# Two-layer model block on one Trainium2 core: weight splits given to GpSimd, convolution accumulated in PSUM

## The reference, cut to what matters

```python
def first_block(x, meta_tokens, ...):            # 512 tokens + 16 meta tokens, D = 1024
    n = _rms(h, norm_mix_w[l])
    z = n @ w_in[l]
    q, k, v, glu, g_att, g_conv = jnp.split(z, splits, axis=-1)
    o = _diff_attention(q, k, v, lam, cid)       # 8 heads, two softmaxes a head
    y_att = _rms(o, subln_w[l]) * (1.0 - lambda_init)
    u = glu[..., :CONV_CH] * jax.nn.sigmoid(glu[..., CONV_CH:])
    u = _causal_dwconv(u, conv_dw_w[l], conv_dw_b[l])       # 31 taps over positions, per channel
    u = jax.nn.silu(_layernorm(u, conv_ln_w[l], conv_ln_b[l]))
    y_conv = u @ w_conv_out[l]
    m = jax.nn.sigmoid(g_att) * y_att + jax.nn.sigmoid(g_conv) * y_conv
    h = h + m @ w_out[l]
    ...                                          # feed-forward part, then second_block
```

## Time and profile before

| what | value |
| --- | --- |
| median of 3 runs | 1806.2 us (1805.16 to 1809.17) |
| the profiled execution's own time | 1807.76 us |
| its span | 1806.0 us |
| PE busy | 1787.0 us (99%), 13222 matmuls |
| PE weight loads busy | 1687.2 us (93%) |
| DVE busy | 1403.3 us (78%) |
| ACT busy | 967.9 us (54%) |
| POOL busy | 164.6 us (9%) |
| granted PE clock over the span | 0.998 |

### The profile page before, as it was taken

The page is one execution under the profiler, slowest core; times in us unless marked ns, Lnnn a source line. Parts: engine busy times, 40 slices in busy tenths (PEclk is TensorE's granted clock), DMA queues, the critical chain, the costliest instruction groups (busy, mean ns, idle before and its releaser), DMA issues.

```text
span 1806.0 us, 31948 instructions
## 1 busy us (share of the span) xinstructions
PE 1787.0 (99%) x13222; PEld 1687.2 (93%) x13222; DVE 1403.3 (78%) x2464; ACT 967.9 (54%) x1894; POOL 164.6 (9%) x138
## 2 busy tenths in 40 slices
PE   9999999999999999999999999999999999999998
PEld 8999999978899989999889999999898999999987
DVE  5888898578756789969878996899357898689844
ACT  6223332568734446547556665667346566566632
POOL 0000000000000012011001211120000122122000
PEclk9999999999999999999999999999999999999999
DMA  5222222200132257566346876785332677577531
GB/s 193 96 75 93 94 86 80 94 24 25 64 107 73 80 136 165 133 160 144 108 117 146 173 159 139 157 170 127 117 94 71 127 167 161 139 156 168 124 117 70
DMA packets 247679, 213.42 MB, mean 118 GB/s; under 512 B 6646, under 2 KB 239919, under 8 KB 247534
## 3 DMA queue, kind: packets, MB, share of 16 engines
q1 hardware_dynamic: 180990, 178.34, 32.2%
q0 software_dynamic: 66528, 33.04, 14.9%
q10 hardware_dynamic: 16, 0.00, 0.0%
HBM read 209.26 MB, written 2.10 MB: 117 GB/s over the span
## 4 chain that ended last, share of the span: by engine, by line
PE 88%; DVE 6%; ACT 4%; DMA 1%; issue 1%; SPq 0%; DVEq 0%; ACTq 0%
PE ps L664 41%; PE ps L705 29%; PE ps L1313 6%; PE ps L1362 5%; DVE wlo L2350 2%; PE ps L893 1%; PE ps L1151 1%; PE ps L1126 1%; ACT p L1624 1%; ACT whi L1396 1%; DMA raw<-in_w_up_dram 1%; PE ps L1142 1%; PE ps L1154 1%; PE ps L918 1%; DVE y L2846 0%
## 5 line engine op out<-in xcount | busy, mean ns | idle before, releaser
L2350 DVE TENSOR_TENSOR wlo<-raw,whi 128x1024 fp32r<-128x1024 f32 (+1 forms) x363 | 438.7, 1214 | 203.9 <-ACT whi L1396 203.0
L1396 ACT ACTIVATE whi<-raw 128x1024 fp32r<-128x1024 f32 (+1 forms) x363 | 380.8, 1052 | 253.3 <-PE ps L664 107.1
L664 PE MATMUL ps<-nhi,whi 128*128 128x256 f32 (+3 forms) x1392 | 315.9, 290 | 1.5 <-DVE clo L2618 0.8
L664 PE MATMUL ps<-nhi,wlo 128*128 128x256 f32 (+3 forms) x1392 | 311.8, 288 | 0.0
L664 PE MATMUL ps<-nlo,whi 128*128 128x256 f32 (+2 forms) x1264 | 275.0, 287 | 0.0
L664 PEld LDWEIGHTS ps<-nhi,whi 128*128 128x128 f32 x1392 | 226.8, 189 | 5.2 <-DVE clo L2618 1.0
L664 PEld LDWEIGHTS ps<-nhi,wlo 128*128 128x128 f32 x1392 | 225.8, 189 | 2.1
L705 PE MATMUL ps<-thi,whi 128*128 128x256 f32 x784 | 225.2, 287 | 2.1 <-DVE wlo L2350 0.7
L705 PE MATMUL ps<-thi,wlo 128*128 128x256 f32 x784 | 221.6, 283 | 0.0
L705 PE MATMUL ps<-tlo,whi 128*128 128x256 f32 x784 | 221.4, 282 | 0.0
L705 PE MATMUL ps<-nhi,whi 128*128 128x256 f32 (+1 forms) x756 | 215.8, 285 | 0.0
(11 more groups left out here) (473 smaller groups left out, 3604.1 us busy)
## 6 DMA issues: line engine op xcount, KB each, us to landing
raw<-in_w_in_dram SPq DMA_DIRECT2D x90, 1024.0 KB, 5.9
raw<-in_w_up_dram SPq DMA_DIRECT2D x22, 1024.0 KB, 5.1
raw<-in_w_out_dram SPq DMA_DIRECT2D x20, 1024.0 KB, 5.1
s1t<-in_w_in_dram SPq DMA_DIRECT2D x49, 256.0 KB, 3.5
s1t<-in_w_in_dram POOLq DMA_DIRECT2D x49, 256.0 KB, 7.1
raw<-in_w_in_dram POOLq DMA_DIRECT2D x49, 256.0 KB, 4.7
raw<-in_w_down_dram SPq DMA_DIRECT2D x16, 512.0 KB, 3.4
raw<-in_w_conv_out_dram SPq DMA_DIRECT2D x4, 1024.0 KB, 5.2
```

The lines of the kernel that those rows point to most:

```text
L664: mm = eng.matmul(o, w, m[:, k, a:b], start=begins, stop=final and n == len(ks) - 1 and i == 2)
L1396: eng.activation(hi, raw, ACT.Copy).then_inc(*A.up("hi", s))
L2350: eng.tensor_tensor(lo, raw, hi.bitcast(F), ALU.subtract).then_inc(*V.up("lo", s))
```

## The change

Two things are done together, with what they need.

1. The subtraction `wlo = raw - whi` of slots 4 to 71 (`BY_GPSIMD`) is issued by POOL in place of DVE. PE and SP wait for POOL's signal there. POOL's three clearing instructions stand between these subtractions: `v` before that of slot 26, the two others before that of slot 58.
2. `conv_steps` keeps its running sum in PSUM banks 6 and 7 for 512 of the 514 positions; the last tap writes the result to `C` in SBUF. The first two positions are computed apart, for two channel blocks together, by two multiplies, one reduction and one addition. The transposed values move to the rotating pairs of banks, and `side.run(6)` becomes `side.run(7)` in the k, v and q tiles.

```diff
+        TAPS, EARLY_SUM = at("taps", [128, 2, 2, 31], F, o_ga + 8704), at("early_sum", [128, 2, 2], F, o_ga + 9728)
...
+        BY_GPSIMD = range(4, next(r for r, (u, _, _) in enumerate(slots) if u == first_ffn))
...
-        for kind in "kvq":
-            in_turn(3, *[(kind, h) for h in range(NH)])
-        turn_of[0] += 1
+        in_turn(3, *[("k", h) for h in range(NH)])
+        in_turn(3, ("v", 0), *[name for h in range(1, NH) for name in (("v", h), ("turn_v", h - 1))])
+        in_turn(3, ("q", 0), ("turn_v", 7), *[("q", h) for h in range(1, NH)])
+        turn_of[0] += 2
...
+        def low_in(s):
+            return G("lo", s) if s in BY_GPSIMD else V("lo", s)
...
                                 if n == c == i == j == 0:
-                                    on.wait_ge(V("lo", s))
+                                    on.wait_ge(low_in(s))
...
+            for n in range(2):
+                emptied([6 + n], V("tap", 6 + n, 30))
...
             def low(s):
+                if s in BY_GPSIMD:
+                    return
...
             def conv_steps(j):
+                fs, early = slice(2 * j, 2 * j + 2), [U[:, 2 * j:2 * j + 2, 14 + e:45 + e] for e in range(2)]
+                for e in range(2):
+                    on.wait_ge(V("u", 2 * j + 1), A("cv"), A("cf"), j and V("early", j - 1))
+                    eng.tensor_tensor(TAPS[:, :, e, :], early[e], cv[:, fs, 0:31], ALU.mult).then_inc(*V.up("early_taps", j, e))
+                yield
...
                 for tap in range(31):
                     for f in (2 * j, 2 * j + 1):
-                        src, c = U[:, f, 14 + tap:14 + tap + TQ], cv[:, f, tap:tap + 1]
+                        src, c = U[:, f, 16 + tap:16 + tap + T2], cv[:, f, tap:tap + 1]
+                        z = bank_dst(6 + f % 2)[0]
...
-                            eng.scalar_tensor_tensor(C[:, f, :], src, c, C[:, f, :], ALU.mult, ALU.add).then_inc(*V.up("tap", f, tap))
+                            eng.scalar_tensor_tensor(z if tap < 30 else C[:, f, 2:TQ], src, c, z, ALU.mult, ALU.add) \
+                                .then_inc(*V.up("tap", f, tap))
...
-                side.run(6)
+                side.run(7)
...
+            for s in BY_GPSIMD:
+                u = slots[s][0]
+                if s == slots.index((12, BY_COL[0], False)) + 2:
+                    on.wait_ge(T("keys"), A("square_x", 0))
+                    eng.memset(V_[:, 0, :], 0.0).then_inc(*G.up("meta"))
...
+                hi, lo, raw = split_views(s)
+                on.wait_ge(A("hi", s))
+                eng.tensor_tensor(lo, raw, hi.bitcast(F), ALU.subtract).then_inc(*G.up("lo", s))
```

More of the change, by code:

```diff
@@ L828, in turn_values @@
             def turn_values(h):
-                src = VT[h % 2]
-                on.wait_ge(A("vt", h), *free(6, 7))
+                src, b = VT[h % 2], 2 * PAIR["turn_v", h]
+                on.wait_ge(A("vt", h), *free(b, b + 1))
                 for t in range(4):
-                    turned = eng.transpose(P[:, 3072 + 128 * t:3200 + 128 * t], src[:, NM + 128 * t:NM + 128 * t + 128], ident)
+                    turned = eng.transpose(P[:, 512 * b + 128 * t:512 * b + 128 * t + 128], src[:, NM + 128 * t:NM + 128 * t + 128], ident)
                 turned.then_inc(*T.up("turn_v", h))
-                eng.transpose(P[0:NM, 3584:3712], src[:, 0:NM], ident).then_inc(*T.up("turn_vm", h))
-                emptied([6], A("v", h))
-                emptied([7], A("vm", h))
+                eng.transpose(P[0:NM, 512 * b + 512:512 * b + 640], src[:, 0:NM], ident).then_inc(*T.up("turn_vm", h))
+                emptied([b], A("v", h))
+                emptied([b + 1], A("vm", h))
             for h in range(NH):
@@ L1552, in turn_values @@
             def turn_values(h):
+                b = 1024 * PAIR["turn_v", h]
                 on.wait_ge(T("turn_v", h))
-                eng.activation(V_[:, 1:5, 128 * h:128 * h + 128], P[:, 3072:3584].rearrange("p (t c) -> p t c", t=4), ACT.Copy) \
+                eng.activation(V_[:, 1:5, 128 * h:128 * h + 128], P[:, b:b + 512].rearrange("p (t c) -> p t c", t=4), ACT.Copy) \
                     .then_inc(*A.up("v", h))
                 on.wait_ge(T("turn_vm", h), G("meta"))
-                eng.activation(V_[0:NM, 0, 128 * h:128 * h + 128], P[0:NM, 3584:3712], ACT.Copy).then_inc(*A.up("vm", h))
+                eng.activation(V_[0:NM, 0, 128 * h:128 * h + 128], P[0:NM, b + 512:b + 640], ACT.Copy).then_inc(*A.up("vm", h))
             for h in range(NH):
@@ L2511, in conv_steps @@
             def conv_steps(j):
+                fs, early = slice(2 * j, 2 * j + 2), [U[:, 2 * j:2 * j + 2, 14 + e:45 + e] for e in range(2)]
[3 more added lines that the diff above has]
+                yield
+                on.wait_ge(V("early_taps", j, 0), V("early_taps", j, 1))
+                eng.tensor_reduce(EARLY_SUM, TAPS, AX.X, ALU.add).then_inc(*V.up("early_sum", j))
+                yield
+                on.wait_ge(V("early_sum", j))
+                eng.tensor_tensor(C[:, fs, 0:2], EARLY_SUM, cv[:, fs, CB:CB + 1].to_broadcast([128, 2, 2]), ALU.add) \
+                    .then_inc(*V.up("early", j))
+                yield
                 for tap in range(31):
                     for f in (2 * j, 2 * j + 1):
-                        src, c = U[:, f, 14 + tap:14 + tap + TQ], cv[:, f, tap:tap + 1]
+                        src, c = U[:, f, 16 + tap:16 + tap + T2], cv[:, f, tap:tap + 1]
+                        z = bank_dst(6 + f % 2)[0]
                         if tap == 0:
-                            on.wait_ge(V("u", f), A("cv"), A("cf"))
-                            eng.tensor_scalar(C[:, f, :], src, c, cv[:, f, CB:CB + 1], ALU.mult, ALU.add).then_inc(*V.up("tap", f, 0))
+                            on.wait_ge(V("u", f), A("cv"), A("cf"), V("tap", f - 2, 30) if j else V("u", 1))
+                            eng.tensor_scalar(z, src, c, cv[:, f, CB:CB + 1], ALU.mult, ALU.add).then_inc(*V.up("tap", f, 0))
                         else:
                             on.wait_ge(V("tap", f, tap - 1))
-                            eng.scalar_tensor_tensor(C[:, f, :], src, c, C[:, f, :], ALU.mult, ALU.add).then_inc(*V.up("tap", f, tap))
+                            eng.scalar_tensor_tensor(z if tap < 30 else C[:, f, 2:TQ], src, c, z, ALU.mult, ALU.add) \
+                                .then_inc(*V.up("tap", f, tap))
                         yield
@@ L2523, in conv_steps @@
                     if f == 1:
-                        on.wait_ge(V("tap", 0, 30), V("tap", 1, 30))
+                        on.wait_ge(V("tap", 0, 30), V("tap", 1, 30), V("early", 0))
                         eng.tensor_tensor(LNS, C[:, 0, :], C[:, 1, :], ALU.add).then_inc(*V.up("sum", 1))
                     elif f > 1:
-                        on.wait_ge(V("sum", f - 1), V("tap", f, 30))
+                        on.wait_ge(V("sum", f - 1), V("tap", f, 30), V("early", f // 2))
                         eng.tensor_tensor(LNS, LNS, C[:, f, :], ALU.add).then_inc(*V.up("sum", f))
@@ L3498, in gpsimd_program @@
             eng.memset(U[:, :, 0:30], 0.0).then_inc(*G.up("pad"))
[L3499 to L3503, removed]
+            for s in BY_GPSIMD:
[3 more added lines that the diff above has]
+                    eng.memset(V_[:, 0, :], 0.0).then_inc(*G.up("meta"))
+                elif s == slots.index((28, BY_COL[0], False)) + 2:
+                    for i in range(2):
+                        on.wait_ge(T("gate", 15))
+                        eng.memset(AT[i][:, 4, :], 0.0).then_inc(*G.up("at_rows", i))
+                hi, lo, raw = split_views(s)
+                on.wait_ge(A("hi", s))
+                eng.tensor_tensor(lo, raw, hi.bitcast(F), ALU.subtract).then_inc(*G.up("lo", s))
             def first_sum(n):
@@ L3556, in first_sum @@
                         on.wait_ge(V("second_sum", sevens[n - 2]), V("lo", slot_of[sevens[n - 2], 1]))
-                    on.wait_ge(V("lo", raw2_read))
+                    on.wait_ge(low_in(raw2_read))
                     eng.dma_start(S1T[n % 2], plan[u][0][:, 0:4, 128:256]).then_inc(*QUARTER_IN[n % 2].up("unit", u))
```

## The result

| | before | after |
| --- | --- | --- |
| median of 4 runs each | 1807.41 us | 1819.25 us |
| lowest to highest | 1805.16 to 1809.17 us | 1816.71 to 1822.72 us |
| profiled execution, its span | 1807.76, 1806.0 us | 1816.71, 1814.9 us |

The ratio is 1.0067, 95% interval 1.0046 to 1.0089: slower by about 12 us, between 8 and 16 by the interval. The forecast was 1818.6 us, 12.4 above the 1806.2 of that time.

The account below looks back on a forecast made before the run. PE alone was taken to set the pace up to about 345 us, then PE, DVE and ACT closely geared in attention. Holds of 9.6 + 1.0 + 1.8 = 12.4 us on 1806.2 gave 1818.6 us, range 1804.0 to 1823.5.

Parts of the forecast that it names:

- The first 345 us, 0: Before attention PE is never idle, so freeing DVE of 54 subtractions and moving the convolution to PSUM gains 0.
- POOL's subtraction, 2.25 us: Duration of one low-part subtraction on POOL, estimated at 2.25 us, between 1.6 and 2.7.
- The disputed term: In attention, POOL's SBUF reads hold DVE's two-input instruction for d = 2.1 us; less 0.5, 1.6 a head, 9.6 for six.
- the room of 0.5: In each attention head, 0.5 us before DVE's reciprocal, won back from the hold because DVE's low part is gone.
- First head 1.0, end 1.8: Hold costs 1.0 us in attention's first head and 0.9 for each of two subtractions at attention's end.
- the sum of 12.4: Total predicted loss in us from holds in attention: 9.6 + 1.0 + 1.8.
- The gain of 0.2 us a head: In attention, DVE without its low part lets PE start 0.2 us sooner a head, 1.2 us for six.
- Taps in PSUM, 0 to 0.1 us: In the convolution, writing the sum to PSUM adds 0 to 0.1 us a tap; effect on the kernel's time 0.
- The moved transposes, 0: Transposed values in rotating bank pairs cost 0: pairs are claimed again two tiles later, copies take under 1 us.
- no hindrance: Rival for attention: POOL and DVE read side by side or lose little; 1805.0 us, the same; chance 0.33.
- POOL as the bound: Rival: POOL's subtraction outlasts a 5.9 us tile, PE waits at 51 slots; at 6.5 us, +31, 1837 us; chance 0.02.
- taps over 1 us: Rival: PSUM taps over 1 us each end after the gates begin their layer norm, so PE waits; chance 0.02.

Follow-up runs that it names:

- the first two experiments: Changed kernel with POOL subtracting only up to slot 57: 1806.97 us, ratio 1.0000; changed kernel with every subtraction on DVE, convolution in PSUM: 1806.27 us, ratio 1.0001.

## Why the prediction was right

- **The first 345 us, 0**: right for the 54 subtractions and for the convolution, and shown by the first two experiments apart. The last tap is 22 us earlier and nobody waited for it.
- **POOL's subtraction, 2.25 us** (between 1.6 and 2.7): 2.40 beside taps, 2.36 in attention. That I came so near is in part luck: I had added a price for each read, and the multiply with one read takes 2.8 us, longer than the subtraction with two, so the instruction's time is not made up in that way. The estimate from the Trainium skill's figure (GPSIMD Engine Reference, section 3.1; 2.2 us for this size) was about as near as mine.
- **The disputed term, d = 2.1 less 0.5 = 1.6 us a head**: right as a mechanism, and 1.5 in size. `ast` is held by 2.03 us; the room of 0.5 shows as the difference between 2.03 a head with DVE's own subtraction kept and 1.5 without it. Of my place for it only this differed: one row takes the whole hold, and the rows behind it run as before.
- **First head 1.0, end 1.8**: 1.5 and 1.3, and that they make up the sum is luck. The 1.5 of the first head are PE's clock, which I had not foreseen; the hold there adds nothing that the trace shows. It can: with taps in SBUF the first head's chain goes through an `ast` of 1.68 us. At the end I charged two subtractions with 0.9 each. One holds `rcol` by 2.17 us (2.33 against 0.16), the other `mlo` by 0.85; the room there was not as I had placed it. So the sum of 12.4 compares with 10.5 us of POOL's.
- **The gain of 0.2 us a head** from a DVE without the low part: measured by itself, 14.65 to 14.46.
- **Taps in PSUM, 0 to 0.1 us**: 0. **The moved transposes, 0**: 0.9 us, once. PE waits 0.67 us for ACT's copy of the last query tile at about 257 us, because the next tile now takes the same pair of banks; the wait is in every kernel with the moved transposes and absent where the transposes stay in banks 6 and 7. It is too small to show in the medians.
- **The rivals**: no hindrance fell by the row of 2.25 us; POOL as the bound by PE's 304.3 busy us of 305; taps over 1 us by the row of 748 ns.

What the prediction lacked was the alternative that a scheduler would look for: in the same head there is a stretch behind the maximum in which DVE reads PSUM or is idle, and the same subtraction costs nothing there. In short: the mechanism of the main term and its size a head (1.6 forecast, 1.5 measured) were right, and the rest of the agreement, 12.4 against 12.05, is two terms that I had left out (0.9 and 1.5 us) and an execution that began 0.85 us earlier.

## What to carry to other kernels

Work taken off an engine under a PE that never idles is worth nothing, however much of it there is: 54 of 68 subtractions moved here without a trace in the time, though they held DVE there too. When elementwise work with SBUF inputs goes to GpSimd, list what VectorE does in the 2.4 us behind its release: a one-column instruction with both inputs in SBUF was held for 2.03 us here, nearly all of the 2.36, so let the GpSimd instruction wait for a point at which VectorE reads PSUM or is idle, or cut it into pieces, which left 0.6 of the 1.5 us a head here. Look for an instruction whose row is ten times its usual length and ends with one of another engine; the median of its group hides it if only some are held. Compare the granted clock stage by stage too, before a difference is charged to the change.

## What the runs showed of the hardware that I had not expected

- POOL's one-input multiply on 128x1024 took 2.8 us, longer than the two-input subtraction (2.37), but held DVE for 0.72 us only.
- An integer `TENSOR_SCALAR` of 128x4, SBUF to SBUF, took 2.24 us beside POOL's subtraction, where it takes 0.17.
- The hold runs both ways: in 40 to 345 us, with taps in SBUF, POOL's subtraction took 2.83 us on average, and one of them 10.3.
- PE's granted clock fell to 0.50 for about 3.4 us in the first head of some executions, the changed kernel's and those of kernels without a subtraction on POOL, and not in others: 1.5 us.
